# Expert layer of a two-layer decoder trunk: 128 tokens by gathered rows and 448 by dense products, instead of 64 and 512

## The reference

```python
def peer_ffn(x, wq, keys, u_tab, v_tab):       # per token; 8 heads, 128 keys a side, top 16
    q = (xb @ wq).reshape(blk, PEER_HEADS, 2, PEER_DK)
    s = jnp.einsum('nhpd,hpkd->nhpk', q, keys)
    s1, i1 = lax.top_k(s[:, :, 0], PEER_TOPK)
    s2, i2 = lax.top_k(s[:, :, 1], PEER_TOPK)
    cand = (s1[..., :, None] + s2[..., None, :]).reshape(blk, PEER_HEADS, PEER_TOPK * PEER_TOPK)
    cidx = (i1[..., :, None] * N_KEYS + i2[..., None, :]).reshape(...)
    sc, pos = lax.top_k(cand, PEER_TOPK)
    idx = jnp.take_along_axis(cidx, pos, axis=-1)
    g = jax.nn.softmax(sc.astype(jnp.float32), axis=-1)
    act = jax.nn.gelu(jnp.einsum('nhkd,nd->nhk', u_tab[idx], xb), approximate=False)
    return jnp.einsum('nhk,nhkd->nd', (g * act).astype(v_tab.dtype), v_tab[idx])
```

## Time and profile before

| | |
|---|---|
| median of 3 runs | 5997.27 us |
| profiled execution | 5996.48 us, span 5994.7 us |
| TensorE matmul, weight load | 5708.6 us (95%), 4859.7 us (81%) |
| VectorE | 3296.9 us (55%) |
| ScalarE | 1910.5 us (32%) |
| GpSimd | 337.5 us (6%) |
| DMA | 905.28 MB, mean 151 GB/s |
| mean granted clock of TensorE | 0.973 |

### The profile page before, as it was taken

The page is one execution under the profiler, slowest core; times in us unless marked ns, Lnnn a source line. Parts: engine busy times, 40 slices in busy tenths (PEclk is TensorE's granted clock), DMA queues, the critical chain, the costliest instruction groups (busy, mean ns, idle before and its releaser), DMA issues. The chain is left out here.

```text
span 5994.7 us, 83802 instructions
## 1 busy us (share of the span) xinstructions
PE 5708.6 (95%) x31410; PEld 4859.7 (81%) x31410; DVE 3296.9 (55%) x6229; ACT 1910.5 (32%) x2798; POOL 337.5 (6%) x266
## 2 busy tenths in 40 slices
PE   8999997999999999999989999979999999999998
PEld 6777776998887888888767777769988878888887
DVE  3453454336887774555434544543378877645554
ACT  2322323223224552222223223232232255522222
POOL 0000000000001111111100000000000011111111
PEclk9999997999999999999999999979999999999999
DMA  3222211224448987666422222112234489876664
GB/s 109 66 62 70 66 48 60 84 87 129 122 130 249 282 269 277 245 245 246 177 100 66 62 70 66 48 65 81 86 129 127 126 257 285 266 276 241 242 246 182
DMA packets 478086, 905.28 MB, mean 151 GB/s; under 512 B 81652, under 2 KB 286516, under 8 KB 459572
## 3 DMA queue, kind: packets, MB, share of 16 engines
q1 hardware_dynamic: 440804, 767.10, 38.9%
q0 software_dynamic: 36992, 134.30, 6.8%
HBM read 733.64 MB, written 169.94 MB: 151 GB/s over the span
## 5 line engine op out<-in xcount | busy, mean ns | idle before, releaser
L1667 PE MATMUL ps<-parts,splits 128*128 128x512 f32 (+1 forms) x7488 | 1617.2, 375 | 3.6 <-DVE ix L2097 3.6
L1667 PEld LDWEIGHTS ps<-parts,splits 128*128 128x128 f32 x7488 | 1323.7, 188 | 236.3 <-issue 4.3
L2223 PE MATMUL ps<-parts,splits 128*128 128x512 f32 x6144 | 1396.5, 390 | 4.4 <-DVEq L2271 4.4
L2223 PEld LDWEIGHTS ps<-parts,splits 128*128 128x128 f32 x6144 | 1155.5, 188 | 245.4 <-DVEq L2271 5.3
L2307 DVE TENSOR_TENSOR splits<-raw,splits 128x1024 fp32r<-128x1024 f32 x250 | 306.3, 1225 | 614.8 <-ACT splits L2258 614.8
L2258 ACT CAST splits<-raw 128x1024 fp32r<-128x1024 f32 x250 | 263.3, 1053 | 961.1 <-PE ps L2223 940.2
L165 PE MATMUL ps<-xn,wr 128*128 128x288 f32 x1952 | 495.6, 408 | 13.0 <-PEq L105 10.6
L2006 DVE TENSOR_TENSOR splits<-raw,splits 128x1024 fp32r<-128x1024 f32 x288 | 352.9, 1225 | 230.9 <-ACT splits L1899 228.2
L165 PEld LDWEIGHTS ps<-xn,wr 128*128 128x128 f32 x1952 | 364.0, 190 | 126.0 <-issue 33.6
L1430 PE MATMUL ps<-parts,wmh 128*128 128x288 f32 x2048 | 414.0, 298 | 27.5 <-DVE parts L1488 27.5
L1430 PEld LDWEIGHTS ps<-parts,wmh 128*128 128x128 f32 x2048 | 330.4, 190 | 29.0 <-issue 29.0
(11 more groups left out here) (401 smaller groups left out, 7810.5 us busy)
## 6 DMA issues: line engine op xcount, KB each, us to landing
raw<-in_u SPq DMA_DIRECT2D x256, 512.0 KB, 4.2
raw<-in_v SPq DMA_DIRECT2D x256, 512.0 KB, 8.8
activated<-go SPq DMA_DIRECT2D x256, 256.0 KB, 4.7
coefficients<-wt SPq DMA_DIRECT2D x32, 2048.0 KB, 10.3
wr<-in_w_cm SPq DMA_DIRECT2D x104, 512.0 KB, 4.3
first<-activated SPq DMA_DIRECT2D x32, 1024.0 KB, 6.0
wb<-coefficients SPq DMA_DIRECT2D x32, 1024.0 KB, 8.2
wt<-activated SPq DMA_DIRECT2D x32, 1024.0 KB, 6.4
```

The costliest lines, as they stand in the source:

```text
L1667: last = nc.tensor.matmul(out, wp[:, slot, k, :], xp[:, k, cols], start=(k == 0 and wp is T.wh and xp is T.xh), stop=(k == KD - 1 and wp i ...
L2223: last = nc.tensor.matmul(out, vp[:, r % 4, m * P:(m + 1) * P], coef, start=(r == 0 and vp is T.vh and gp is T.xh), stop=(ends and vp is T ...
```

## The change

The 64 last prompt tokens join the gathered ones. The gathered side now has one token per partition (`NG` = 128), the sample tokens on partitions 0 to 63 and prompt tokens 448 to 511 on the others, and 128 gathers a table instead of 64; the dense side has `ND` = 448 columns. Beats fall to 56, and the search takes 80 tiles, 10 per head. The dot products with u are spread over three places: 56 in the search (8 in each head from the second on, with rows that earlier heads found), 42 in the beats (three of four beats), 30 in the first ten blocks of the value stage (three per block). In the value stage a blend follows every row. The sums of pairs shrink from 256 to 65 candidates (pair a, b can be in the top 16 only if a x b is at most 16; the set is covered by four bands of 16 and one more), and the index arithmetic is rewritten in f16 with sums by halving. The gather indices are formed per head; the copies over partitions go.

```diff
-NG = NS
+NG = P
...
-PER = 9
-U_STATIC = 7 * PH_HEADS
+PER = 10
+U_STATIC = 8 * PH_HEADS
...
-SLOTS = PH_HEADS * TOPK * NG // P
+SLOTS = PH_HEADS * TOPK
 GRING = 4
+EARLY_DOTS = 8 * (PH_HEADS - 1)
+BRING = 3
+BEAT_DOTS = 2 * BRING * (CHUNKS // 2)
+LATE_DOTS = SLOTS - EARLY_DOTS - BEAT_DOTS
+LATE_PER = 3
...
+LEVELS_CAND = 4
+NCAND = LEVELS_CAND * TOPK + 1
...
-            pool.wait_ge(s["indexed"], 2)
-            pool.dma_start(T.gidx[NG:P, 0:SLOTS], T.gidx[0:NG, SLOTS:2 * SLOTS]).then_inc(s["moved_i"], 16)
-            pool.dma_start(T.gw[NG:P, :], T.found[0:NG, 2, TILES - 1, SLOTS:2 * SLOTS]).then_inc(s["moved_w"], 16)
-            pool.wait_ge(s["moved_i"], 16)
-            for j in range(SLOTS):
+            pool.wait_ge(s["x_out"], 16)
+            for j in range(EARLY_DOTS):
+                if j % TOPK == 0:
+                    pool.wait_ge(s["indexed"], j // TOPK + 1)
                 if j >= GRING:
                     pool.wait_ge(s["dotted"], j - GRING + 1)
-                gather_rows(nc, T, T.d["u_rows"], j).then_inc(u_in[j % GRING], 16)
-            pool.wait_ge(s["moved_w"], 16)
+                gather_rows(nc, T, T.d["u_rows"], j, T.ge[j % GRING]).then_inc(e_in[j % GRING], 16)
+            pool.wait_ge(s["indexed"], PH_HEADS)
+            for j in range(BEAT_DOTS):
+                if j >= BRING:
+                    pool.wait_ge(s["dotted"], EARLY_DOTS + j - BRING + 1)
+                gather_rows(nc, T, T.d["u_rows"], EARLY_DOTS + j, T.gt[j % BRING]).then_inc(u_in[j % BRING], 16)
...
+            act.wait_ge(s["dotted"], EARLY_DOTS)
...
-                nc.vector.tensor_copy(T.xdup[:, k], T.scaled[:, k % 4, ND:N].unsqueeze(1).to_broadcast([P, 2, NG])
-                                      ).then_inc(s["x_dup"], 1)
+                nc.vector.tensor_copy(T.xdup[:, k, 0], T.scaled[:, k % 4, SEQ:N])
+                nc.vector.tensor_copy(T.xdup[:, k, 1], T.scaled[:, k % 4, ND:SEQ]).then_inc(s["x_dup"], 1)
...
+            def early_dots(first, count):
+                for j in range(first, first + count):
+                    dve.wait_ge(e_in[j % GRING], 16 * (j // GRING) + 16)
+                    v.scalar_tensor_tensor(
+                        out=T.ge[j % GRING], in0=T.ge[j % GRING], scalar=1.0, in1=T.xrow, op0=ALU.mult, op1=ALU.mult,
+                        accum_out=T.gact[:, j:j + 1]).then_inc(s["dotted"], 1)
...
+                    if dots is not None:
+                        early_dots(dots + 2 * r, 1)
...
+            def pair_sums():
+
+                side = T.t1.rearrange("p (t z) a -> p t z a", z=2)
+                for level in range(LEVELS_CAND):
+                    a, b = 1 << level, TOPK >> level
+                    shape = [P, TILES, a, b]
+                    v.tensor_tensor(
+                        T.cand[:, :, level * TOPK:(level + 1) * TOPK].rearrange("p t (a b) -> p t a b", a=a),
+                        side[:, :, 0, a - 1:2 * a - 1].unsqueeze(3).to_broadcast(shape),
+                        side[:, :, 1, 0:b].unsqueeze(2).to_broadcast(shape), ALU.add)
+                link(v.tensor_tensor(T.cand[:, :, NCAND - 1:NCAND], side[:, :, 0, TOPK - 1:TOPK], side[:, :, 1, 0:1],
+                                     ALU.add))
+
+            def pair_places():
+
+                v.tensor_scalar(T.lev, T.posu, 4, None, ALU.logical_shift_right)
+                link(v.tensor_scalar(T.rest, T.posu, 15, 16, ALU.bitwise_and, ALU.bitwise_or))
+                link(v.tensor_tensor(T.rest, T.rest, T.lev, ALU.logical_shift_left))
+                v.tensor_scalar(T.place[:, 0], T.rest, 4, None, ALU.logical_shift_right)
+                link(v.tensor_scalar(T.rest, T.rest, 15, None, ALU.bitwise_and))
+                link(v.tensor_tensor(T.place[:, 1], T.rest, T.lev, ALU.logical_shift_right))
+                link(v.tensor_copy(T.twin, T.place.rearrange("p z t k -> p (z t k)").unsqueeze(2).to_broadcast(
+                    [P, ROWS, 2])))
+
+            def indices(h, n):
+
+                eq = T.eq.rearrange("p (x a) -> p x a", a=TOPK)
+                side = ROWS // 2
+                shape = [P, side, TOPK // 2, 2]
+                for z in range(2):
+                    rows = slice(z * side, (z + 1) * side)
+                    marks = T.marks[:, z, :].rearrange("p (a two) -> p a two", two=2)
+                    last = v.tensor_tensor(eq[:, rows].rearrange("p x (a two) -> p x a two", two=2),
+                                           T.twin[:, rows].unsqueeze(2).to_broadcast(shape),
+                                           marks.unsqueeze(1).to_broadcast(shape), ALU.is_equal)
+                link(last)
+                lows(n, 1)
+                eq4 = T.eq.rearrange("p (x k a) -> p x k a", k=TOPK, a=TOPK)
+                link(v.tensor_tensor(eq4, eq4, T.i1f.unsqueeze(2).to_broadcast([P, 2 * TILES, TOPK, TOPK]), ALU.mult))
+                half = TOPK // 2
+                while half > 1:
+                    link(v.tensor_tensor(eq[:, :, 0:half], eq[:, :, 0:half], eq[:, :, half:2 * half], ALU.add))
+                    half //= 2
+                ends = T.eq.rearrange("p (x k a) -> p a x k", k=TOPK, a=TOPK)
+                link(v.tensor_tensor(T.found[:, 0:2, :, h * TOPK:(h + 1) * TOPK].rearrange("p z t k -> p (z t) k"),
+                                     ends[:, 0], ends[:, 1], ALU.add))
+                lows(n + 1, 1)
+
             for h in range(PH_HEADS):
                 ending = h == PH_HEADS - 1
                 n = LEAD + 1 + PER * h
                 dve.wait_ge(s["kept"], 2 * h + 4)
                 n = best(T.t1, T.i1u, T.scr[:, h % 2].rearrange("p t z k -> p (t z) k"), n,
-                         (1, 1, 1, 0) if ending else (1, 1, 1, 1))
+                         (1, 1, 1, 0) if ending else (1, 1, 1, 1), 8 * (h - 1) if h else None)
                 dve.sem_inc(s["topped"], 1)
-                nc.vector.tensor_copy(T.i1f, T.i1u)
-                side = T.t1.rearrange("p (t z) a -> p t z a", z=2)
...
-                n = best(T.tv, T.posu, T.cand, n, (1, 0, 1, 0) if ending else (1, 1, 1, 0))
-                nc.vector.tensor_copy(T.t2[:, :, h, :], T.tv)
-                nc.vector.tensor_scalar(T.pau, T.posu, 4, None, ALU.logical_shift_right)
-                link(nc.vector.tensor_scalar(T.pbu, T.posu, 15, None, ALU.bitwise_and))
-                nc.vector.tensor_copy(T.paf, T.pau)
-                link(nc.vector.tensor_copy(T.pbf, T.pbu))
-                sidei = T.i1f.rearrange("p (t z) a -> p t z a", z=2)
-                eq = T.cand.rearrange("p t (k a) -> p (t k) a", a=TOPK)
-                eq4 = T.cand.rearrange("p t (k a) -> p t k a", a=TOPK)
-                for z, place in enumerate((T.paf, T.pbf)):
-                    link(nc.vector.tensor_tensor(eq, flat(place).unsqueeze(2).to_broadcast([P, TILES * TOPK, TOPK]),
-                                                 iota, ALU.is_equal))
-                    link(nc.vector.tensor_tensor(eq4, eq4, sidei[:, :, z, :].unsqueeze(2).to_broadcast(shape), ALU.mult))
-                    link(nc.vector.tensor_reduce(T.found[:, z, :, h * TOPK:(h + 1) * TOPK], eq4, AX_X, ALU.add))
-                    lows(n, 1)
-                    n += 1
+                v.tensor_copy(T.i1f.rearrange("p (z t) a -> p t z a", z=2), T.i1u.rearrange("p (t z) a -> p t z a", z=2))
+                pair_sums()
+                n = best(T.t2[:, :, h, :], T.posu, T.cand, n, (1, 1, 1, 0) if ending else (1, 1, 1, 1),
+                         8 * (h - 1) + 4 if h else None)
+                pair_places()
+                indices(h, n)
+                n += 2
+                cols = slice(h * TOPK, (h + 1) * TOPK)
+                for rows, t in ((slice(0, NS), TILES - 1), (slice(NS, P), TILES - 2)):
+                    last = v.scalar_tensor_tensor(out=T.idxf[rows, cols], in0=T.found[rows, 1, t, cols],
+                                                  scalar=float(NKEY), in1=T.found[rows, 0, t, cols],
+                                                  op0=ALU.mult, op1=ALU.add)
+                link(last)
+                v.tensor_scalar(T.gidx[:, cols], T.idxf[:, cols], T.base, None, ALU.add).then_inc(s["indexed"], 1)
...
+                j = EARLY_DOTS + 2 * BRING * cc + BRING * i + b
...
-                        dot(cc, i, b)
+                        if b < BRING:
+                            dot(cc, i, b)
...
+        LATE_BLOCKS = LATE_DOTS // LATE_PER
+        LATE_AT = {1: 0, 4: 1, 6: 2}
...
+                gather_rows(nc, T, table, j, T.gt[j % GRING]).then_inc(rows_in[j % GRING], 16)
+                p, x = divmod(j, BLOCK)
+                if p < LATE_BLOCKS and x in LATE_AT:
+                    q = LATE_PER * p + LATE_AT[x]
+                    if q >= LATE_PER:
+                        pool.wait_ge(s["dotted"], q - LATE_PER + 1)
+                    gather_rows(nc, T, T.d["u_rows"], SLOTS - LATE_DOTS + q, T.gu[q % LATE_PER]
+                                ).then_inc(late_in[q % LATE_PER], 16)
...
```

(29 more changed lines are left out.)

128 lines of the change are left out of this document (68 added, 60 removed).

## The result

Measured on one chip beside the kernel before (5995.81 us): 5760.15 us, the median of four runs from 5751.90 to 5768.48; ratio 0.9605, 95% interval 0.9594 to 0.9617. Forecast were 5669 us and a range of 5645 to 5735, so the direction was right and the time is outside the range: 236 us gained, not 327. The profiled execution took 5768.48 us, 5766.8 of them its span, which is 100 us over the sum of 5668.5.

What follows compares the result with a forecast made beforehand. TensorE, busy for 95% of the span, was taken as the bound. From 5996.5 us, narrower matmuls (-331), fewer sums (-16) and small costs of 2 x 9.5 us gave 5668.5, so 5669; range 5645 to 5735.

Steps and rivals of the forecast that it cites:

- The step that failed: Value stage: v loads issued seven rows (33 us, less some 6) ahead need 8.8 us to land, so no loss.
- late rows: Value stage: rows that come late because the DMA engines are nearly full, 2 us a layer.
- The pitch: Dense products of lookup and value stage: 199.6 ns per matmul at 448 columns instead of 226.5, 331 us off.
- a floor by weight loads: Rival on the dense matmuls: weight loads keep 448 columns near 226 ns, so no change at 5998 us; chance 0.01.
- The sums: Beats: 16 small sums take 1.00 us of each; 8 fewer beats a layer take 16 us off in all.
- VectorE in the search: Search: VectorE's work per head rises from 44.5 to 48.2 us of 53.3, worst case 52.7, and stays hidden.
- its rival: VectorE bounds the search: at 56 us per head, +50 us, 5720 in all; chance 0.09.
- The end of the search: Last head of the search: TensorE's wait for VectorE grows by 2.3 us a layer (0.4 less to 6 more).
- the start of the lookup: Lookup's first products: a copy in each of 8 steps lengthens VectorE's scaling and splitting chain, 0.9 us a layer.
- The value stage's start: First value-stage rows: extra gathers behind the residual's load cost 4 us a layer, bounds 0 to 14.
- DMA engines' pace: Rival: DMA engines set the pace in the value stage's first 80 rows, 5690 to 5735 us; chance 0.18.
- GpSimd: Value stage: 1.4 gathers a row at 2.28 us, held by VectorE's instructions, take 3.1 of 4.79 us, no loss.

Runs made afterwards that it cites:

- v_first: The changed kernel with the value stage's 1.8 MB of activations and coefficients issued after the v loads they stood ahead of: 5697.75 us, ratio 0.9497.
- w_on_act: The changed kernel with the value stage's activations and coefficients loaded by ScalarE's queue, so SyncE's carries v alone: 5687.31 us, ratio 0.9489.
- before_448_v: The kernel before, dense matmuls narrowed to 448 columns, activations and coefficients issued after the v loads of rows 3 and 7: 5712.11 us, ratio 0.9523.
- hold_only2: The changed kernel, v loads of rows 2 and 6 still held for the fourth low part, but the 1.8 MB issued after the v loads: 5700.54 us.
- v_first_h: The changed kernel with the 1.8 MB issued after the v loads and the residual's load moved to the last block: 5685.14 us, ratio 0.9486.
- no_late: The changed kernel without the value stage's 30 late dot products per layer, their gathers and Gelu (weights set to zero): 5761.91 us, ratio 0.9609.
- widths_act: The changed kernel with dense products of 384 columns (lookup) and 320 (value stage), activations and coefficients on ScalarE's queue: 5327.10 us, one execution.
- widths: The changed kernel with dense products narrowed to 384 columns in the lookup and 320 in the value stage: 5604.84 us, one execution.

## Why the prediction was wrong

- **The step that failed** is the sentence "A v load is issued when row x is split, three rows ahead of TensorE, and is for row x + 4: seven rows, 33 us, less some 6 for the two splits, and it needs 8.8 now" with its "Twice the present times would still be hidden". That is true of v loads in rows 0 and 1. Those of rows 2 and 3 (6 and 7) stand in SyncE's program behind a wait for the weighed activations' low parts and behind 1.8 MB. I counted seven rows of slack where a loop of 20.9 us had 0.9. The rows for it were in the trace of before: the same queue, and a landing of 8.8 us for 0.5 MB while 392 GB/s flow, which is 1.3 us of transfer. Shown by v_first, w_on_act, before_448_v and hold_only2. Of the 100 us it is 54: from start to start the 50 waits of the two value stages take 66.4 us more than the pitch, less the 12 that I had allowed for late rows and the start. (The profile's idle time for them is 58.2: it begins at a matmul's end, 0.37 us after its start, where the next start was due after 0.20.) The loop costs more than its waits: in w_on_act's profiled run the two value stages are 83 us shorter together, since the matmuls between waits are 205.1 ns apart on average here and 202.7 there.
- **The pitch** was a mis-sized term: 199.6 ns forecast from the line through 288 and 512 columns, 202.7 or 206.7 measured. In the lookup the distance between the 3072 dense matmuls of a layer fell by 24.8 ns on average (229.4 to 204.6 over all neighbouring pairs in the trace), 76 us and not 82.6. In the value stage, at 205.1 on average between waits, 5.5 x 3072 = 17 us a layer are missing. In both layers that is another 46 us, 14 of them by the cadences that stand between waits, as said above. That the line holds elsewhere (173 ns at 384 columns, where it gives 172.6; 147 at 320, 145.7) makes the misfit one of 448 and not of the reasoning on a floor by weight loads, for which nothing speaks.
- **The sums**: a beat takes 5.85 us (5.79 forecast, the difference is the pitch), 8 fewer are worth 8 us a layer. Right.
- **VectorE in the search**: heads come every 53.84 us (53.3), VectorE is busy for 256.6 of 300, 46 us per head (48.2 forecast, 52.7 the worst case). Right, and its rival is refuted: no wait of TensorE for a low part there.
- **The end of the search**: 4.17 + 0.37 us and 1.7 ahead of the indices (3.72 + 1.80 before), so +0.7 and not +2.3. Together with the start of the lookup (+0.1 for 0.9) 2.4 us a layer cheaper than forecast.
- **The value stage's start**: one wait of 4.41 us at 2239.98, in the forecast's 4 with bounds of 0 to 14. In w_on_act it is gone, with the residual still at its place; in v_first 1.7 us are left, and moving the residual away takes them too (v_first_h); in hold_only2 it is 4.8. So the wait needs the shared queue, but the residual has a part in it, and the hold may have one as well.
- **The rival "DMA engines' pace"** had the right place and a range that ends 25 us short of the median, but not the mechanism. By it, the pace would follow the traffic; no_late took 13% of it away and nothing moved, and in w_on_act 352 GB/s flow in the same rows without a wait of TensorE. At 320 columns the rival comes true (widths_act). My test for it, TensorE idle "in front of in_v ... all along those blocks", could not tell it from the loop; the last six blocks could.
- **GpSimd**: a gather of v rows takes 1.49 us on average where those of the search take 0.99 and those of the beats 1.26 (I had set 2.28), and GpSimd is busy for 39% of the windows above at most. The Trainium skill (GPSIMD Engine Reference, section 1 Specifications) says that GpSimd shares its SBUF interface with VectorE, in contention with instructions of two SBUF inputs. The trace agrees: of the 128 gathers into second, 56 meet no such instruction of VectorE in their first 0.99 us and take 0.99, the other 72 take 1.88. In the search VectorE is busier (256.6 of 300 us), but 82 of the 112 gathers meet only its scans of one input, and they take 0.99. It costs nothing here.
- **DMA limit**: the Trainium skill (DMA: Bandwidth & Descriptors, Bandwidth) gives about 358 GB/s as the limit of a core's HBM transfers. I left out that the same section calls this each core's part when both cores of an HBM domain stream; this kernel runs on one core. Measured are 382 over 100 us with TensorE full (v_first), and 411 at a share of 1.02 (widths_act). The measurement decides.

The two terms of 54 and 46 us, 5 less for the small costs, make 95 of the 100. Another 2 are matmuls at the lower granted clock right after a wait (373 ns apart, see below), and some 3 stay open. Not resolved: what selects one of the two cadences, and why the line through 288 and 512 columns misses at 448.

## What to carry to other kernels

Before you narrow the work of the bounding engine, write down the loops that don't pass through it: a queue's program, what stands ahead in it in bytes, what its wait hangs on, and the period that results. Here that period was 20.9 us under a bound of 21.8, and no share, mean or median slack shows it; the short, urgent load belongs ahead of the large one, or in another queue. And when a narrowing brings less than its count of columns says, look at whether the period has a fixed length in rows of the loop: it was the same at 448 and at 320.

## What the runs showed of the hardware

- Matmuls of 448 columns with a weight load each have two cadences at the same granted clock of 1.00: 202.7 ns (a repeating pattern of 199 to 207) and 206.7. Two layers of one execution differ in it (v_first, with the same instructions and loads), and it can change between two waits (the changed kernel, after 2399.6). The 14 us between v_first's own runs are about what one stage's cadence makes; that it is the reason is not shown.
- In the first value stage a 0.5 MB load landed 13.7 us after its issue (median) where 1.8 MB stood ahead in its queue, 5.9 with the order turned (v_first, hold_only2) and 6.5 with the 1.8 MB in ScalarE's queue (w_on_act), at equal or higher traffic (331 GB/s, and 352 in v_first and w_on_act, from 2300 to 2400). With 288 GB/s and the old order it still took 13.4 (no_late). Here a queue's order counted for more than its rate.
- With waits of mostly 4 to 5 us in every 21 the granted clock fell: widths has 0.85 from 2300 to 2400, and 96 matmuls of 320 columns after such a wait took 16.63 us (173 ns each), while 192 of them in widths_act took 28.40 (148). Where the waits were mostly 1 to 2 us, in the changed kernel, its windows above show 1.00. It isn't the length of the wait alone: of this kernel's 50 waits, three (4.41, 3.81 and 2.24 us) were followed by 8 to 10 matmuls 373 ns apart, the pace of the 1.2 GHz level for 448 columns, and others of up to 2.46 us were not. So in widths the loop costs some clock as well, but hides that too.

```profile
2220.80 16.63 PE L2303 MATMUL ps<-parts,splits 128*128 128x320 f32 x96 [4.39 <-DVE parts L2361]
```
```profile
2584.16 28.40 PE L2298 MATMUL ps<-parts,splits 128*128 128x320 f32 x192 [1.37 <-DVE parts L2363]
```
